# Second mixer: row sums with ones as the stationary operand in four column tiles, and places by half units for layer norm, attention and head norms

## The reference

```python
u = ua * jax.nn.sigmoid(ub)
u = lax.conv_general_dilated(u, conv_w, ...) + conv_b      # 31 taps, each channel for itself
u = jax.nn.silu(layer_norm(u, conv_ln_g, conv_ln_b))
y_conv = u @ conv_w_out + conv_b_out
...
att = causal_diff_attention(q1, q2, k1, k2, v, lam)        # 8 heads, 512 queries in 4 blocks of 128
y_att = rms_norm(att, head_norm) * (1.0 - lam_init)        # mean square over the 128 values of a head
g_conv, g_att = jnp.split(jax.nn.sigmoid(gate_logits), 2, axis=-1)
y = (g_conv * y_conv + g_att * y_att) @ w_o
x = x + g1 * rms_norm(y, post_norm1)
```

## Time and profile before

| | |
|---|---|
| median of three runs | 2729.72 us (2728.4 to 2731.86) |
| the profiled execution | 2732.39 us |
| its span, first to last instruction | 2730.6 us |
| TensorE (PE) busy | 2622.6 us, 96% |
| VectorE (DVE) busy | 1458.6 us, 53% |
| ScalarE (ACT) busy | 930.7 us, 34% |
| GpSimd (POOL) busy | 1118.8 us, 41% |
| mean granted TensorE clock | 0.972 |
| DMA | 253.41 MB, mean 93 GB/s |

### The profile page before, as it was taken

How to read it: one execution, slowest core, us unless ns; L and a number is a source line. 1 busy time by engine, 2 the same in 40 slices (tenths; PEclk the granted TensorE clock), 3 DMA queues, 4 the chain that set the end, 5 groups by cost and what they waited for, 6 DMA issues and landing times. The chain is left out here.

```text
span 2730.6 us, 32363 instructions
## 1 busy us (share of the span) xinstructions
PE 2622.6 (96%) x12740; PEld 2084.9 (76%) x12740; DVE 1458.6 (53%) x1805; ACT 930.7 (34%) x1318; POOL 1118.8 (41%) x503
## 2 busy tenths in 40 slices
PE   7999999999999999999999999899989898699997
PEld 6777778788888887778788888687776676588886
DVE  8875435743334895425753333798535663533333
ACT  5333443322223432443422222343334533322222
POOL 4334334344443533334344443378722232344442
PEclk9999999999999999999999999899989989799998
DMA  5223222433334322222343332332211102123331
GB/s 176 70 63 89 70 78 85 138 125 123 123 108 149 89 59 81 78 70 93 101 143 128 126 127 93 107 98 74 84 54 47 47 31 93 61 95 96 96 97 50
DMA packets 226763, 253.41 MB, mean 93 GB/s; under 512 B 9168, under 2 KB 203088, under 8 KB 226384
## 3 DMA queue, kind: packets, MB, share of 16 engines
q1 hardware_dynamic: 226320, 251.19, 29.4%
q10 hardware_dynamic: 320, 0.52, 0.1%
HBM read 246.96 MB, written 4.19 MB: 92 GB/s over the span
## 5 line engine op out<-in xcount | busy, mean ns | idle before, releaser
L218 POOL TENSOR_TENSOR sb_w_lo<-sb_raw,sb_w_hi 128x1024 fp32r<-128x1024 f32 x402 | 981.3, 2452 | 1401.8 <-ACT sb_w_hi L213 1399.9
L213 ACT ACTIVATE sb_w_hi<-sb_raw 128x1024 fp32r<-128x1024 f32 x404 | 422.8, 1057 | 608.9 <-PE ps L242 529.2
L240 PE MATMUL ps<-sb_a_hi,sb_w_hi 128*128 128x512 f32 x1472 | 606.0, 412 | 21.5 <-DVE sb_w_lo L218 10.3
L241 PE MATMUL ps<-sb_a_lo,sb_w_hi 128*128 128x512 f32 x1472 | 588.2, 400 | 0.0
L242 PE MATMUL ps<-sb_a_hi,sb_w_lo 128*128 128x512 f32 x1472 | 587.8, 399 | 0.0
L240 PE MATMUL ps<-sb_b_hi,sb_w_hi 128*128 128x512 f32 x960 | 382.7, 399 | 8.1 <-PEq L190 4.4
L241 PE MATMUL ps<-sb_b_lo,sb_w_hi 128*128 128x512 f32 x960 | 381.4, 397 | 0.0
L242 PE MATMUL ps<-sb_b_hi,sb_w_lo 128*128 128x512 f32 x960 | 381.0, 397 | 0.0
L240 PEld LDWEIGHTS ps<-sb_a_hi,sb_w_hi 128*128 128x128 f32 x1472 | 280.8, 191 | 119.4 <-issue 36.1
L242 PEld LDWEIGHTS ps<-sb_a_hi,sb_w_lo 128*128 128x128 f32 x1472 | 280.4, 191 | 68.5
L241 PEld LDWEIGHTS ps<-sb_a_lo,sb_w_hi 128*128 128x128 f32 x1472 | 281.5, 191 | 64.3 <-issue 2.4
(11 more groups left out here) (376 smaller groups left out, 2880.5 us busy)
## 6 DMA issues: line engine op xcount, KB each, us to landing
sb_raw<-in_w_in_dram SPq DMA_DIRECT2D x148, 512.0 KB, 3.7
sb_raw<-in_w_ffn_in_dram SPq DMA_DIRECT2D x88, 512.0 KB, 5.1
sb_raw<-in_w_ff_dram SPq DMA_DIRECT2D x64, 512.0 KB, 3.8
sb_ada<-in_w_ada_dram SPq DMA_DIRECT2D x48, 512.0 KB, 4.6
sb_raw<-in_w_ffn_out_dram SPq DMA_DIRECT2D x44, 512.0 KB, 3.8
sb_raw<-in_w_mix_o_dram SPq DMA_DIRECT2D x16, 512.0 KB, 3.4
sb_raw<-in_w_conv_o_dram SPq DMA_DIRECT2D x8, 512.0 KB, 3.5
sb_raw<-in_w_attn_o_dram SPq DMA_DIRECT2D x8, 512.0 KB, 3.4
```

The lines of the kernel that those rows point to most:

```text
L213: act.activation(w_hi[:, s, :], raw[:, s, :], ACT.Copy).then_inc(hi_done[s], 1)
L218: pool.tensor_tensor(w_lo[:, s, :], raw[:, s, :], w_hi[:, s, :].bitcast(F32), ALU.subtract)\
L240: pe.matmul(out, wh, hi, start=first and i == 0, stop=False)
L241: pe.matmul(out, wh, lo, start=False, stop=False)
```

## The change

The one-column sums are replaced by `sum_parts`: 32 columns of ones are the stationary operand, a data tile of 512 tokens the moving one, and tile n writes to the 32 PSUM partitions from 32 x (n % 4) on. Four tiles stand side by side in the array, a second four are added onto the first. The result is a row of sums over tokens in each group of 32 partitions. ScalarE copies it to SBUF (`KEEP_AT`). For the mean of the layer norm one matmul with `pick` (1/1024 at partitions 0, 32, 64 and 96) adds the four rows and spreads the result at once; for the squares four matmuls with `pick` as the moving operand give four columns again; for the heads four matmuls against four columns of the identity give sixteen columns, four heads by four blocks.

The places move:

- Sums of the layer norm: (18, 0) with the spread at (18, 2); squares (19, 3), their columns (20, 1), spread (20, 3) into the bank `SUM_BANK`. GpSimd's root goes from before unit 42's remainder to before unit 43's.
- Scaling of the layer norm in pairs of tiles from (20, 3), tanh in pairs from (21, 1), gating in pairs from (22, 0), products in pairs from (27, 2).
- Attention steps from (21, 1), heads from (28, 2).
- Head sums in two parts: (29, 2) and (30, 2); columns (30, 0) and (31, 0); spreads at (30, 3) for heads 0 and 1, (31, 0) for 2 and 3, (31, 3) for 4 to 7, with VectorE's scaling at the same places. Product remainders 0 to 3 of wo go to (31, 3), the rest behind group 31.
- New waits: `values(0)` for `ln_ready`, ScalarE's copies for `parts`, their readers for `part_kept`.

```diff
+def halves_from(gi, half, values):
+    return {divmod(HALVES * gi + half + n, HALVES): v for n, v in enumerate(values)}
+STEPS_AT = {at: [i] for at, i in halves_from(LN_AT + 3, 1, range(N_STEPS)).items()}
+HEADS_AT = halves_from(at2[("cv", 0)], 2, range(HEADS2))
+CENTRED_AT = halves_from(LN_AT + 2, 3, [range(n, n + 2) for n in range(0, KD, 2)])
+TANH_AT = halves_from(LN_AT + 3, 1, [range(n, n + 2) for n in range(0, KD, 2)])
+GATED_AT = halves_from(LN_AT + 4, 0, [range(n, n + 2) for n in range(0, KD, 2)])
+PRODUCTS_AT = halves_from(at2[("ga", 3)], 2, [range(n, n + 2) for n in range(0, KD, 2)])
+CV3 = at2[("cv", 3)]
+SPREADS_AT = {(CV3 - 1, 3): range(0, 2), (CV3, 0): range(2, 4), (CV3, 3): range(4, 8)}
+HEAD_BANK = [4, 6, 4, 6, 5, 7, 4, 6]
+KEEP_AT = {(LN_AT, 1): (0, SUM_BANK), (LN_AT + 1, 3): (1, SUM_BANK), (CV3 - 2, 3): (2, 4), (CV3 - 1, 3): (3, 5)}
...
+pick = small[:, 22:23]
+of_parts = [sq[:, 7, :], sq[:, 0, :], k[:, 0, :], k[:, 1, :]]
...
-if un == 2 * (LN_AT + 3):
+if un == 2 * (LN_AT + 3) + 1:
     pool_rsqrt(pool, 1)
-if un == 2 * at2[("wo", 1)]:
-    pool_rsqrt(pool, 2, width=32)
+if un in (2 * CV3 + 2, 2 * CV3 + 4):
+    r = (un - 2 * CV3 - 2) // 2
+    these = slice(16 * r, 16 * r + 16)
+    pool.wait_ge(mean_done, 3 + r)
+    pool.tensor_tensor(rstd[:, these], rstd[:, these], neg_half[:, these], ALU.pow)\
+        .then_inc(rstd_done, 1)
...
+def sum_parts(src, tiles, bank):
+    for n, kt in enumerate(tiles):
+        g = slice(32 * (n % 4), 32 * (n % 4) + 32)
+        ins = pe.matmul(ps[g, bank, :], ones[:, 0:1].to_broadcast([P, 32]), src[:, kt, :],
+                        start=n < 4, stop=n >= len(tiles) - 4)
+    ins.then_inc(parts, 1)
+def head_parts(r, bank):
+    pe.wait_ge(squares, KD + 4 * r + 4)
+    pe.wait_ge(exps_done, 2 * len(ITEMS2))
+    sum_parts(conv, range(4 * r, 4 * r + 4), bank)
+def head_columns(r, bank):
+    pe.wait_ge(part_kept, 3 + r)
+    for n in range(NB):
+        ins = pe.matmul(ps[:, bank, 4 * n:4 * n + 4], of_parts[2 + r][:, n * P:(n + 1) * P],
+                        ident[:, 0:P:32], start=True, stop=True)
+    ins.then_inc(sums_done, 1)
...
-if gi == LN_AT:
-    pe.wait_ge(conv_done, 16)
-    pe.wait_ge(rope_sin, 16)
-    pe_sum(pe, conv, SUM_BANK, n_sq=KD)
-if gi == LN_AT + 2:
-    pe_sum(pe, sq, SUM_BANK, squares, KD, n_sq=KD)
-if name == "wo" and p == 0:
-    pe.wait_ge(rstd_kept, 1)
-    for hd in range(HEADS2):
-        if hd >= 4:
-            pe.wait_ge(heads_done, hd - 3)
+for half in range(HALVES):
+    if (gi, half) == (LN_AT, 0):
+        pe.wait_ge(conv_done, 16)
+        pe.wait_ge(rope_sin, 16)
+        sum_parts(conv, range(KD), SUM_BANK)
+    if (gi, half) == (LN_AT, 2):
+        pe.wait_ge(part_kept, 1)
+        pe.matmul(ps[:, SPREAD_BANK, :], pick.to_broadcast([P, P]), of_parts[0], start=True, stop=True)\
+            .then_inc(spread, 1)
+    if (gi, half) == (LN_AT + 1, 3):
+        pe.wait_ge(squares, KD)
+        sum_parts(sq, range(KD), SUM_BANK)
+    if (gi, half) == (LN_AT + 2, 1):
+        pe.wait_ge(part_kept, 2)
         for n in range(NB):
-            i = hd * NB + n
-            ins = pe.matmul(ps[:, 4 + hd % 4, n * P:(n + 1) * P],
-                            rstd[:, i:i + 1].to_broadcast([P, P]), ident[:, :], start=True, stop=True)
-        ins.then_inc(spread, 1)
-for half in range(HALVES):
+            ins = pe.matmul(ps[:, SUM_BANK, n:n + 1], of_parts[1][:, n * P:(n + 1) * P], pick,
+                            start=True, stop=True)
+        ins.then_inc(sums_done, 1)
+    if (gi, half) == (LN_AT + 2, 3):
+        pe_spread(pe, rstd, SUM_BANK, rstd_done, 1)
     i, o = half // 2, half % 2
     for s in STEPS_AT.get((gi, half), []):
         slot(s)
-    if gi == at2[("cv", 3)] and half == 1:
-        pe.wait_ge(squares, 2 * KD)
-        pe.wait_ge(o_hi, len(ITEMS2))
-        for item, (hd, n) in enumerate(ITEMS2):
-            ins = pe.matmul(ps[:, 4, item:item + 1], conv[:, hd, n * P:(n + 1) * P], ones[:, 0:1],
-                            start=True, stop=True)
-        ins.then_inc(sums_done, 1)
+    if (gi, half) == (CV3 - 2, 2):
+        head_parts(0, 4)
+    if (gi, half) == (CV3 - 1, 0):
+        head_columns(0, 6)
+    if (gi, half) == (CV3 - 1, 2):
+        head_parts(1, 5)
+    if (gi, half) == (CV3, 0):
+        head_columns(1, 7)
+    for hd in SPREADS_AT.get((gi, half), []):
+        spread_head(hd)
...
+if (gi, half) in KEEP_AT:
+    n, bank = KEEP_AT[gi, half]
+    if n == 2:
+        act.wait_ge(s_max, len(ITEMS2))
+    act.wait_ge(parts, n + 1)
+    act.activation(of_parts[n], ps[:, bank, :], ACT.Copy).then_inc(part_kept, 1)
...
+for kt in TANH_AT.get((gi, half), []):
+    act.wait_ge(ln_ready, kt + 1)
+    lt.done(act.activation(ln_tanh[:, kt, :], conv[:, kt, :], ACT.Tanh, scale=0.5))
+for kt in PRODUCTS_AT.get((gi, half), []):
+    multiplied(act, 2 * at2[("ga", 3)] + kt // 4)
+    prod_round(h_hi[:, kt, :], conv[:, kt, :], 0.5)
+if (gi, half) == (CV3, 3):
+    multiplied(act, 2 * CV3)
+    for kt in range(4):
+        prod_round(h_hi[:, kt, :], gc[:, kt, :], 0.5)
...
+for kt in CENTRED_AT.get((gi, half), []):
+    step.done(stt(conv[:, kt, :], conv[:, kt, :], pcol("conv_ln_g", kt),
+                  ps[:, SUM_BANK, :], ALU.mult, ALU.mult))
+    lr.done(ts(conv[:, kt, :], conv[:, kt, :], pcol("conv_ln_b", kt), None, ALU.add))
+for kt in GATED_AT.get((gi, half), []):
+    dve.wait_ge(ln_th, kt + 1)
+    pready.done(stt(conv[:, kt, :], ln_tanh[:, kt, :], 1.0, conv[:, kt, :], ALU.add, ALU.mult))
+for kt in PRODUCTS_AT.get((gi, half), []):
+    prod_rest(kt, conv[:, kt, :])
+if (gi, half) == (CV3 - 1, 0):
+    head_means(0, 6)
+if (gi, half) == (CV3 - 1, 2):
+    head_roots(0)
+if (gi, half) == (CV3, 0):
+    head_means(1, 7)
+if (gi, half) == (CV3, 2):
+    head_roots(1)
+for hd in SPREADS_AT.get((gi, half), []):
+    if hd == 4:
+        for kt in range(4):
+            prod_rest(kt, gc[:, kt, :])
+    head_normed(hd)
+    if hd < 6:
+        pready.done(tt(gc[:, hd, :], gc[:, hd, :], ga[:, hd, :], ALU.add))
...
+if gi == CV3 and o:
+    for kt in (4, 5):
+        prod_rest(kt, gc[:, kt, :])
...
+    if gi == CV3:
+        for hd in (6, 7):
             pready.done(tt(gc[:, hd, :], gc[:, hd, :], ga[:, hd, :], ALU.add))
-            if hd:
-                prod_rest(hd - 1, gc[:, hd - 1, :])
-        prod_rest(HEADS2 - 1, gc[:, HEADS2 - 1, :])
+            prod_rest(hd, gc[:, hd, :])
 dve_add_squares(dve, step, conv, 2 * KD, 0)
 dve_mean(dve, SUM_BANK, 4, cm)
 dve.wait_ge(spread, 3 + HEADS2 + 1)
```

More of the change, by code:

```diff
@@ L485, in build @@
         ln_th = sem("ln_th")
-        ln_mean = sem("ln_mean")
+        parts = sem("parts")
+        part_kept = sem("part_kept")
         glu_done = sem("glu_done")
@@ L2226, in values @@
                                 pe.wait_ge(o_hi, i)
+                            else:
+                                pe.wait_ge(ln_ready, KD)
                             for b in range(n + 1):
@@ L2238, in slot, with spread_head @@
                                 scores(i)
+                        def sum_parts(src, tiles, bank):
[14 more added lines that the diff above has]
+                            ins.then_inc(sums_done, 1)
+                        def spread_head(hd):
+                            pe.wait_ge(rstd_kept, 1 + hd // 4)
+                            bank = HEAD_BANK[hd]
+                            if hd == 0:
+                                pe.wait_ge(part_kept, 3)
+                            elif hd == 1:
+                                pe.wait_ge(o_hi, len(ITEMS2))
+                            elif hd == 4:
+                                pe.wait_ge(part_kept, 4)
+                            elif hd in (2, 3):
+                                pe.wait_ge(heads_done, hd - 1)
+                            elif hd in (6, 7):
+                                pe.wait_ge(heads_done, hd - 3)
+                            for n in range(NB):
+                                i = 16 * (hd // 4) + 4 * n + hd % 4
+                                ins = pe.matmul(ps[:, bank, n * P:(n + 1) * P],
+                                                rstd[:, i:i + 1].to_broadcast([P, P]), ident[:, :], start=True, stop=True)
+                            ins.then_inc(spread, 1)
                         for gi, (name, p) in enumerate(G2):
@@ L2396, in _ @@
                                     act.activation(tap_prod[m], src, ACT.Identity, scale=w, bias=bias).then_inc(tap_made, 1)
+                            if gi == LN_AT + 1:
+                                for kt in range(KD):
+                                    act.wait_ge(centred, kt + 1)
+                                    act.activation(sq[:, kt, :], conv[:, kt, :], ACT.Square).then_inc(squares, 1)
                             for half in range(HALVES):
+                                if (gi, half) in KEEP_AT:
[4 more added lines that the diff above has]
```

(27 more changed lines are left out.)

63 lines of the change are left out of this document (18 added, 45 removed).

## The result

| | before | after |
|---|---|---|
| median of the runs, us | 2730.44 (2728.4 to 2731.86, 4 runs) | 2696.44 (2695.13 to 2697.36, 4 runs) |
| profiled execution, us | 2732.39 | 2697.19 |
| its span, us | 2730.6 | 2695.3 |

The ratio is 0.9875 (95% interval 0.9861 to 0.9888): 34.0 us faster where I expected 50, and 3.4 us above the top of my range.

What follows compares the result with a forecast made beforehand. TensorE was taken as the bound, busy 2622.6 of 2730.6 us. A to E sum to 49.9 us, taken from 2732.4 to give 2682.5; the median lies 2.7 lower, so about 2680 us, range 2672 to 2693.

Steps and rivals of the forecast that it cites:

- A: First layer-norm sums: 12.0 us lost to one-column matmuls and slow multiplies; the new form should win 10.2 us.
- B: Second layer-norm sums: 12.2 us lost in the same way; new sums plus return to columns should win 9.2 us.
- rival 1: New sums: the four column tiles don't overlap; price 11.4 us, 2691 us; chance 0.12.
- C: Start of attention, steps 0 to 3: 12.4 us lost; earlier steps and VectorE work in pairs should win 9.9.
- D: Attention step at the products for cv: 8.3 us lost, 4.33 idle for VectorE's combine; should win 7.5 us.
- E: Head norms and wo 0: 25.9 us lost, 12.8 with the new sums, including 0.9 of wait; 13.1 won.
- The second: VectorE's queue: layer-norm and gated pairs delay every maximum, with GpSimd collisions and a clock fall; 2691.5 us; chance 0.15.
- The third: The losses of 2.5, 0.8 and 0.9 us and switching come to nothing: 2675 us; chance 0.11, or better.
- the fourth: Slower: in all 20 half units with such pieces TensorE's clock stays at 1.2 GHz between steps; 2740 us; chance 0.01.

Runs made afterwards that it cites:

- ln_sums_only: Kernel before the change with only its two layer-norm sums in the new form, every place as before; 2710.73 us, ratio 0.993.
- one_tile: The changed kernel with both eight-tile layer-norm sums in column group 0, one after another, instead of four groups side by side; 2702.56 us.
- hold_c: The changed kernel with GpSimd's remainder of unit 46, at the start of attention, waiting until two gated products are done; 2691.93 us.
- hold_cd: hold_c, with GpSimd's remainders of units 58 and 59 also waiting for four and eight product remainders; 2687.29 us.
- hold_all: hold_cd, with GpSimd's remainders of units 63 to 66 also waiting for VectorE's work and GpSimd's second root moved forward; 2686.65 us.
- best: hold_all, with VectorE adding tiles 6 and 7 ahead of remainders in cv 3's tail and ScalarE rounding product tiles before weight units; 2684.83 us.

## Why the prediction was wrong

- **A and B held.** Each eight-tile sum costs 1.86 us where I took 1.5 + 0.2, the columns 0.81 where I took 1.3, and the multiplies behind keep their pace. ln_sums_only gives 20.0 us for A and B in the runs (19.4 forecast). Two readings of mine were off all the same. One record of 512 columns is not 0.33 us: in one_tile sixteen of them, one after another, take 6.99 us at a granted clock of 1.00, 0.44 each. So my upper bound of 5.3 us should have been 7.0, and by my own formula rival 1 should have been priced at 16.5 us and not 11.4. And the Trainium skill (TensorE: Matmul & The Clock Gate, "Measured speedup vs the span model") has 2.38 times for three column tiles, from which I had worked out an estimate of 2.2 us per sum. No run here has three tiles; four come to 3.8 times.
- **The step that failed is "I leave 2.5 us in C (9.9 won) and 0.8 in D (7.5 won)".** C won 7.7 us and D 2.4, which is 7.3 of the 14.6 us between forecast and trace. The step rested on a price for one collision of VectorE with GpSimd, 1.9 us of VectorE's time, of which the free 2.0 us per step would carry a part. Two things were missing. First, I priced the delay and not its effect on the clock: the delayed step shows 1.8 us of idle, after which the granted clock is 0.59 for the next 7.5 us (windows of the kernel after, here the scores and multiplies of C and of D):

```profile
2014.10:2021.60 7.50, 7.50 (x17) 4.38 (x18) 4.11 (x9) 5.12 (x10) 0.00 (x0) 0.59 0.00 0
2147.60:2155.80 8.20, 8.18 (x18) 4.77 (x19) 4.58 (x9) 5.09 (x11) 0.00 (x0) 0.58 0.00 0
```

  The delayed step costs 4.5 us in C (hold_c) and 4.8 in D (10.55 against 5.71, hold_cd), two thirds of it the clock. The kernel as a whole loses 3.3 and 4.3 us by it, since the steps behind have no wait then; my price was 2.5 us per pair. This price has a scatter, too: in one_tile the same two steps lose 1.6 us less each. Second, my working for D names no collision, though the order of ScalarE's queue makes one likely: a weight unit's rounding releases GpSimd's remainder, and the product tiles stand right behind that rounding. It happened at both steps of the products (3.08 us at 2141.52, 3.11 at 2156.52), and the first is the one that cost time.
- **The rule in the prediction got too little weight.** Here VectorE's instructions with their tiles in SBUF only, when they met GpSimd's remainder, ended with it or up to 0.6 us behind it, and one with a PSUM operand beside the same remainder took its usual time (L2683, 0.75 us at 2008.34). With the rule of the Trainium skill (SBUF — State Buffer, "Who interferes with whom": the shared ports are an exclusive lock, and an instruction with at most one SBUF input outside the two-port modes stays clear) the trace agrees for L2683 and for the product remainders, which have two SBUF inputs. L2685 has one, and would have to run in a two-port mode; no run here shows whether it does. I used the rule for C only and kept 2.5 us; C lost 2.2 more.
- **E cost about 17 us, not 12.8.** Sums (0.99 and 1.00), columns (0.81 twice) and spreads (1.70, 1.79 and 3.49) make 10.6 us, less than my 11.9. But I had no term for waits among them: 1.22, 0.77, 0.47 and 1.12 us are shown, of which 0.77 was there before. In wo 0 there are 2.17 us of wait, not 0.9, and then eight slow multiplies, 1.6 us. hold_all took away the 1.12 us, 0.62 us of the waits in wo 0 and the slow multiplies; the turns that VectorE and ScalarE take in wo 0 are a question of order, which best shows. I had counted VectorE's ten instructions there and said "about 8.6 us together", but not that the last two tiles go one after the other, 2.18 us each.
- **The rest of the miss.** Of the 14.6 us another 3.3 lie ahead of the stretch and behind it, where my sum had nothing and other profiles of these kernels differ by as much.
- **With the collisions out the sum nearly comes true, partly by luck.** By the stretch, I had put the change at 364.2 - 49.9 = 314.3 us; it came out at 325.6, and hold_all at 315.2, best at 312.8. Of the 11.3 us in between the holds of GpSimd's remainders gave back 10.4. But by terms it is a balance: with the hold, step 0 to step 4 takes 18.13 us (hold_cd, 1999.16 to 2017.29), so that C won 12.2 us where I had said 9.9, and D and E together 17.2 where I had said 20.6. And no kernel reached 2680 us: best took 2684.83.
- **The rivals.** The first, no overlap, is refuted. The second, VectorE's queue with GpSimd's collisions and a fall of the clock as in C, is the one whose kind came; I gave it 0.15 and priced it at 2691.5. Its working was not what happened, though: it had all four pairs of C late, and one was, and it had nothing for D's collision or E's waits. The third, no losses, did not come. No half unit stayed slow into the next step, as the fourth needed.
- **What stays open.** The waits of 1.2 and about 1 us in the last attention steps, why the same wait is followed by a slow stretch of different length from profile to profile, and why the code ahead of the stretch took 1951.4 to 1956.6 us (in best's it is 1956.56).

## What to carry to other kernels

When VectorE's work is cut up to fit between the steps of another engine, look at what GpSimd will be doing in that place: a collision delays VectorE by about the rest of GpSimd's instruction, and holding one GpSimd instruction back gave 3.3 us of the stretch here (4.5 by the medians). Look where the held instruction lands, too: it met others of VectorE's there (0.55 us for 0.17, 1.17 for 0.43). Price a wait of TensorE with the slow multiplies behind it, as the trace shows them after waits of that length, not by its idle time. And when two engines hand tiles to each other, write both queues out next to each other; placing two additions before the remainders took 1.2 us of wait away for no work.

## What the runs showed of the hardware that I had not expected

- Four f32 column tiles with 512 moving columns each run at 3.8 times the rate of one (1.86 us against 6.99 for 16 records). Going to that form and back shows no idle; the multiply behind takes 0.34 us until the next, for 0.23.
- TensorE's clock fell from full behind single idles of 1.79 and 1.81 us, and behind 0.95 and 1.22 us only 2.2 us apart; it held behind a single one of 1.31 us and behind 0.33 and 1.22.
- How long it stayed down differs behind the same idle: 1.79 us were followed by a step of 10.47 us in the change and of 8.92 in one_tile (5.95 at full clock with a wait of 0.40, hold_c).
